# A two-model stack on one Trainium2 core: the RWKV inverses and their transposes part ways, and the mixers get new orders

## What is computed

```python
for l in range(DEPTH):                                   # DEPTH = 2
    h = rmsnorm(x, norm_g[l])
    proj = h @ w_in[l]                                   # all inputs of the three mixers
    y_a = hgrn2_mixer(a_q, a_ff, a_fb, a_i, ...) * silu(a_g)
    y_b = retention_mixer(b_q, b_k, b_v, ...) * silu(b_g)
    y_c = rwkv7_mixer(c_s, ...) * silu(c_g)
    mixed = gates_a * (y_a @ w_branch_a[l]) + gates_b * (y_b @ w_branch_b[l]) + gates_c * (y_c @ w_branch_c[l])
    x = x + mixed @ w_out[l]
```

```python
sa = einsum("bhvk,bhk->bhv", S, -kk_t)
S  = S * w_t + sa * (kk_t * a_t) + v_t * k_t
o  = einsum("bhvk,bhk->bhv", S, r_t)
```

## Time and profile before

| | |
|---|---|
| runs before | 3254.1, 3262.1, 3264.2 us, median 3262.1 |
| profiled execution, first to last instruction (span) | 3255.5 us |
| PE busy | 3046.9 us (94%) |
| DVE, ACT, POOL busy | 1688.1, 695.8, 260.2 us |
| chain that ended last, share on PE | 82% |

### The profile page before, as it was taken

How to read it: one execution, slowest core, us unless ns; L and a number is a source line. 1 busy time by engine, 2 the same in 40 slices (tenths; PEclk the granted TensorE clock), 3 DMA queues, 4 the chain that set the end, 5 groups by cost and what they waited for, 6 DMA issues and landing times.

```text
span 3255.5 us, 45292 instructions
## 1 busy us (share of the span) xinstructions
PE 3046.9 (94%) x18996; PEld 2523.1 (78%) x18996; DVE 1688.1 (52%) x3491; ACT 695.8 (21%) x1346; POOL 260.2 (8%) x326
## 2 busy tenths in 40 slices
PE   8989997989999989998899999999989979997999
PEld 7878886878886878887778887895759659764794
DVE  3556646355311564655555420773347557646575
ACT  3223423232111333323133110200110021013100
POOL 1201121020000121202012000000000000000000
PEclk9999998999999999999999999999989989996999
DMA  5323322324333423332233334444325425521343
GB/s 212 105 79 127 94 90 93 116 85 121 117 134 134 128 73 115 94 106 107 68 107 114 118 106 169 140 171 156 130 94 170 167 84 169 172 98 69 134 170 124
DMA packets 153754, 395.56 MB, mean 122 GB/s; under 512 B 90288, under 2 KB 106800, under 8 KB 109648
## 3 DMA queue, kind: packets, MB, share of 16 engines
q1 hardware_dynamic: 51376, 367.94, 32.6%
q10 hardware_dynamic: 100608, 19.93, 3.2%
q0 software_dynamic: 1568, 4.79, 0.4%
HBM read 380.04 MB, written 12.59 MB: 121 GB/s over the span
## 4 chain that ended last, share of the span: by engine, by line
PE 82%; DVE 10%; DMA 5%; ACT 2%; issue 1%; ACTq 1%; POOL 0%; DVEq 0%; SPq 0%
PE bank L418 25%; PE bank L1924 17%; PE bank L1942 7%; PE bank L1748 6%; PE bank L435 5%; PE bank L1811 4%; PE bank L1351 2%; DMA xT_scratch<-rw_bm 1%; PE bank L1953 1%; DMA rw_ex<-xT_scratch 1%; PE bank L731 1%; PE bank L750 1%; DVE rw_ex L662 1%; DVE rw_scored_a L1166 1%; DMA scores_scratch<-rw_scored_a 1%
## 5 line engine op out<-in xcount | busy, mean ns | idle before, releaser
L418 PE MATMUL bank<-h_features,weight_ring 128*128 128x256 f32 x4256 | 974.3, 385 | 10.8 <-DMA weight_ring<-in_w_in 4.8
L418 PEld LDWEIGHTS bank<-h_features,weight_ring 128*128 128x128 f32 x4256 | 805.0, 192 | 125.5 <-issue 6.1
L435 PE MATMUL bank<-weight_ring,h_features 128*128 128x256 f32 (+2 forms) x896 | 201.2, 375 | 3.1 <-DVE h_features L510 2.0
L435 PEld LDWEIGHTS bank<-weight_ring,h_features 128*128 128x128 f32 x896 | 161.9, 190 | 27.3 <-issue 2.3
L1924 PE MATMUL bank<-h_features,weight_ring 128*128 128x128 f32 x1408 | 171.9, 275 | 5.4 <-DVE h_features L510 5.4
L1924 PEld LDWEIGHTS bank<-h_features,weight_ring 128*128 128x128 f32 x1408 | 164.3, 192 | 6.1 <-DVE h_features L510 6.1
L1993 ACT COPY mem_normed<-bank 128x128 f32<-128x128 f32 x88 | 23.4, 265 | 482.7 <-PE bank L1924 482.7
L1748 PE MATMUL bank<-y_features,weight_ring 128*128 128x256 f32 x512 | 119.0, 382 | 0.0
L2076 DVE TENSOR_TENSOR mem_normed<-mem_normed,bank 128x256 f32<-128x256 f32 x88 | 37.0, 421 | 132.5 <-PE bank L1924 132.5
L1748 PEld LDWEIGHTS bank<-y_features,weight_ring 128*128 128x128 f32 x512 | 95.1, 190 | 13.0 <-issue 0.7
L1924 PE MATMUL bank<-y_rwkv_features,y_features 128*128 128x128 f32 x704 | 93.0, 275 | 0.0
(11 more groups left out here) (521 smaller groups left out, 4990.3 us busy)
## 6 DMA issues: line engine op xcount, KB each, us to landing
weight_ring<-in_w_in SPq DMA_DIRECT2D x146, 1024.0 KB, 4.9
weight_ring<-in_f00w SPq DMA_DIRECT2D x33, 1024.0 KB, 4.9
weight_ring<-in_f01w SPq DMA_DIRECT2D x33, 1024.0 KB, 4.8
weight_ring<-in_f10w SPq DMA_DIRECT2D x33, 1024.0 KB, 4.8
weight_ring<-in_f11w SPq DMA_DIRECT2D x33, 1024.0 KB, 4.9
weight_ring<-in_w_b SPq DMA_DIRECT2D x16, 1024.0 KB, 5.0
weight_ring<-in_w_out SPq DMA_DIRECT2D x16, 1024.0 KB, 4.9
weight_ring<-in_conv_in SPq DMA_DIRECT2D x10, 1024.0 KB, 4.9
```

Source lines behind the costliest of these rows:

```text
L418: m = e.matmul(bank[:, j, :], w[:, k, j * P:(j + 1) * P], x[:, k, :], start=k == 0, stop=k == kt - 1, skip_group_check=True)
L435: m = e.matmul(bank[:, t * n:(t + 1) * n], x[:, k, t * P:(t + 1) * P], w[:, k, :], start=k == 0, stop=k == kt - 1, skip_group_check=True)
```

## The change

Three things change.

1. The transposes get semaphores of their own (`rw_xT_stored_sem`, `rw_xT_sem`, and `rw_x_stored_sem`, `rw_x_sem` for the inverses), and `x` and `xT` swap their buffers: `x` is loaded into `rw_ex`, out of which it was stored, and `xT` into `rw_bm`. So neither exchange waits for the other.
2. Store and loads of the transposes leave ACT's queue for SP's, as a fourth stream X in SP's order. L741 (now L742) waits for them; L731 waits for `x` alone.
3. All orders of both mixers' stages are replaced, on five engines; both layers now have the same one. The second block's orders stay.

```diff
-    R.prod, R.x, R.xT = (flat(z).rearrange("p (n s) -> p n s", s=HALF_ROWS) for z in (R.sig, R.bm, R.ex))
+    R.prod, R.x, R.xT = (flat(z).rearrange("p (n s) -> p n s", s=HALF_ROWS) for z in (R.sig, R.ex, R.bm))
...
         if lv == BLOCK:
-            e.wait_ge(g.rw_inverse_sem, 64 * ((4 * l + q) * 2 + d + 1))
+            e.wait_ge(g.rw_x_sem, 32 * ((4 * l + q) * 2 + d + 1))
...
             e.wait_ge(*act.at("prod", *U, lv))
+            e.wait_ge(g.rw_xT_sem, 32 * ((4 * l + q) * 2 + d + 1))
             for i, rows in parts:
...
+def rwkv_inverse_sp(e, g, l):
+    S, R = g.rw, g.R
+    for q in range(4):
+        for d in range(2):
+            unit = (4 * l + q) * 2 + d
+            e.wait_ge(*S.dve.at("inverse", l, q, d))
+            e.wait_ge(g.rw_zeros_sem, 32)
+            if unit:
+                e.wait_ge(g.rw_xT_sem, 32 * unit)
+            e.dma_start(scratch_blocks(g.xT_scratch), block_rows(R.inv)).then_inc(g.rw_xT_stored_sem, 16)
+            yield
+            e.wait_ge(g.rw_xT_stored_sem, 16 * (unit + 1))
+            for half, rows in enumerate(ROW_HALVES):
+                e.dma_start(R.xT[rows], scratch_halves(g.xT_scratch, half)).then_inc(g.rw_xT_sem, 16)
             yield
...
-                e.wait_ge(g.rw_inverse_sem, 64 * unit)
-            e.dma_start(scratch_blocks(g.x_scratch), block_rows(R.inv_tmp)).then_inc(g.rw_stored_sem, 16)
-            e.dma_start(scratch_blocks(g.xT_scratch), block_rows(R.inv)).then_inc(g.rw_stored_sem, 16)
-            yield
-            e.wait_ge(g.rw_stored_sem, 32 * (unit + 1))
-            for z, scratch in ((R.x, g.x_scratch), (R.xT, g.xT_scratch)):
-                for half, rows in enumerate(ROW_HALVES):
-                    e.dma_start(z[rows], scratch_halves(scratch, half)).then_inc(g.rw_inverse_sem, 16)
+                e.wait_ge(g.rw_x_sem, 32 * unit)
+            e.dma_start(scratch_blocks(g.x_scratch), block_rows(R.inv_tmp)).then_inc(g.rw_x_stored_sem, 16)
+            yield
+            e.wait_ge(g.rw_x_stored_sem, 16 * (unit + 1))
+            for half, rows in enumerate(ROW_HALVES):
+                e.dma_start(R.x[rows], scratch_halves(g.x_scratch, half)).then_inc(g.rw_x_sem, 16)
...
         weave(g, f"mixers{l}", "sync", {
             "R": chain(rwkv_sp(e, g, l), branch_sp(e, g, l, 2, "w_c", 1)),
+            "X": rwkv_inverse_sp(e, g, l),
```

Of the order table one line, SyncE's of layer 0, as it now reads at its start:

```diff
-        "H R4 H4 B6 H5 R4 B6 H5 B5 R4 B H B H B H B H B H B3 R4 B4 H2 B H B2 H B H B H B H2 B R8 ",
+        "R4 H5 B5 X2 B H4 R X2 R3 B H B7 X2 B2 H2 X2 R4 H2 B H B4 X B2 X B H2 R X2 R3 H3 B7 X2 B6 H2 X H X2 R2 H "
```

More of the change, by code:

```diff
@@ L218 @@
     ("mixers0", "gpsimd"):
-        "H R3 H11 R H5 R2 H16 R H9 R2 H7 R H11 R2 H5 R ",
+        "H R3 H9 R H7 R2 H9 R H7 R2 H7 R H9 R2 H10 R H7 ",
     ("mixers1", "gpsimd"):
-        "R H R2 H11 R H5 R2 H16 R H10 R2 H6 R H11 R2 H5 R ",
+        "H R3 H9 R H7 R2 H9 R H7 R2 H7 R H9 R2 H10 R H7 ",
     ("mixers0", "sync"):
-        "H R4 H4 B6 H5 R4 B6 H5 B5 R4 B H B H B H B H B H B3 R4 B4 H2 B H B2 H B H B H B H2 B R8 ",
+        "R4 H5 B5 X2 B H4 R X2 R3 B H B7 X2 B2 H2 X2 R4 H2 B H B4 X B2 X B H2 R X2 R3 H3 B7 X2 B6 H2 X H X2 R2 H "
+        "R H R H R H R H2 R3 ",
     ("mixers1", "sync"):
-        "R4 H5 B6 H5 R4 B6 H5 B5 R4 B H B H B H B H B H B3 R4 B6 H4 B2 H B H2 B H B R8 ",
+        "R4 H5 B5 X2 B H4 R X2 R3 B H B7 X2 B2 H2 X2 R4 H2 B H B4 X B2 X B H2 R X2 R3 H3 B7 X2 B6 H2 X H X2 R2 H "
+        "R H R H R H R H2 R3 ",
     ("conv", "sync"):
@@ L3115, in __init__ @@
             nc.dram_tensor(n, (TT * 4 * HEAD_STRIDE,), F32).ap() for n in ("scores_scratch", "x_scratch", "xT_scratch"))
-        self.rw_scores_sem, self.rw_blocks_sem, self.rw_stored_sem, self.rw_inverse_sem, self.rw_zeros_sem = (
-            self.sem(n) for n in ("scores_stored", "blocks_loaded", "inverses_stored", "inverses_loaded",
-                                  "scratch_cleared"))
+        self.rw_scores_sem, self.rw_blocks_sem, self.rw_zeros_sem = (
+            self.sem(n) for n in ("scores_stored", "blocks_loaded", "scratch_cleared"))
+        self.rw_x_stored_sem, self.rw_x_sem, self.rw_xT_stored_sem, self.rw_xT_sem = (
+            self.sem(n) for n in ("inverses_stored", "inverses_loaded", "transposes_stored", "transposes_loaded"))
         self.vectors_sem, self.masks_sem = self.sem("vectors_loaded"), self.sem("masks_loaded")
```

## The result

The changed kernel takes 3293.95 us (median of 14 runs, 3280.94 to 3306.31), the kernel before 3266.73 us (14 runs, 3254.11 to 3286.69) on the same chips. The ratio is 1.008, with a 95% interval of 1.006 to 1.0099. The forecast was 3244 us. The time lies outside the forecast range too, 12 us above its upper end.

A forecast was written before the change was run, and what follows sets the result against it. PE was taken as the bound, busy 3046.9 of 3255.5 us. Stalls at L731 (-8), matmuls laid elsewhere (+2) and fewer changes of run (-3) gave -9 us a layer, -18 in all: 3244 us, range 3216 to 3282.

The forecast's parts named there:

- for those some 4 us it can't start a weight load: SP's queue: waiting for the inversion keeps weight loads off the inverse's store or load, taken as 2.0 us a unit.
- Term A: PE's stalls at L731: from 31.9 to 23.9 us a layer as the chain shortens, -8 us a layer.
- slower rival: Exchange: only issue time is saved, no collision spared; chain 25.1 us, kernel at 3272; chance 0.23.
- The clock ... 0, with 5 us either way.: PE's half clock: two stretches a layer before, three shorter ones after; effect 0, with 5 us either way.
- Term A's base: Modelled stalls at L731 before, with a chain of 27.5 us: 31.9 us a layer.
- term B: Matmuls laid elsewhere: other waits end, -13.4 us, against a new hole and thinner cover, +15; +2 us a layer.
- The new hole: Unit q = 1, d = 1, at L835: PE stalls 9.7 to 12.7 us for operands, taken as 11.
- ACT's 48 issues fewer: ACT's queue: 31 us of issue time less wins nothing, since ACT's waits hide it.
- three signs of being wrong: Loads of `x` landing after 5 us in half the units; L742 waiting; HGRN2 waiting on DVE over 10 us a layer.
- The planner's case: Exchange: transfers near their medians, chain 21.1 us, L731 stalls 13.5 us a layer, kernel at 3224; chance 0.17.

The follow-up runs named there:

- e1: Kernel before with the new orders alone, the exchange still joint and on ACT's queue: 3359.42 us, ratio 1.0285.
- e11: Changed kernel plus one wait on SP's queue, behind the transposes' loads, until the inverses' loads have landed: 3235.47 us, ratio 0.9905.
- e9: Changed kernel, transposes on ACT's queue, SP waiting until the inverses are loaded, one weight load ahead of the transposes' store's old place: 3210.61 us, ratio 0.9826.
- e4: Changed kernel with idle-filling matmuls, 49 a layer ahead of L731's waits and 30 ahead of two HGRN2 waits: 3280.75 us, ratio 1.0039.
- e7: Changed kernel with the loads of w_in after the tenth cut to a sixteenth, so its weights are wrong: 3218.16 us, ratio 0.9853.
- e10: Changed kernel with transposes on ACT's queue, before's orders, and SP waiting at the inversion's place until the inverses are loaded: 3240.54 us, ratio 0.9916.
- e8: Changed kernel with transposes on ACT's queue and SP waiting, where the transposes' store stood, until the inverses are loaded: 3213.84 us, ratio 0.9836.

## Why the prediction was wrong

The sum said -18 us; the span says +47.3 (by the medians, 3244 was forecast and 3293.95 measured, a miss of 50 us; the rest is the spread named above). Of the miss of 65 us, 42 are busy time (36.1 more in the two stages where -6 was forecast), 25 idle time (12.9 more where -12 was forecast), and -2 lie outside the stages.

**The step that failed: "for those some 4 us it can't start a weight load".** Term A rested on 2.0 us a unit of spared collisions. None was spared: 14 of 16 units are hit, for 7.0 us, where it was 12 and 5.4. The sum took the exchange from 9.1 to 4.7 us; measured, it went from 11.5 to 10.8. From the scores to L731 it is 25.6 us, 2.2 less than before, but only 0.7 of that is the exchange. Another 0.9 lies ahead of the inversion's end (15.6 us from the scores before, 14.7 after, 14.6 in e1 with the old exchange), and 0.6 is that PE now starts L731 as soon as `x` lands. So the slower rival's chain (25.1) is near by its number, and its argument from the Trainium skill (DMA: Bandwidth & Descriptors, Issuing engines are not separate DMA queues) held in that no collision was spared; but more and slower collisions ate most of the 2.4 us of issue time too. I looked at where SP waits, and not at when its wait ends against when `x` lands: 3 us after the inversion against 10.8. e11 and e9 show that keeping weight loads away does shorten the exchange: with the wait it takes 9.3 and 6.6 us, and the scores to L731 24.1 and 22.3.

**"The clock ... 0, with 5 us either way."** The largest error in size: 35 us. Up to some 20 of them are the spread of single executions. I priced the half clock by counting two stretches a layer before; the clock record of before has eight in layer 0 and seven in layer 1. The new orders put a wait at L731 into all 16 units and a hole of 11.9 us into both layers, and the time at the lower level nearly doubled (116 to 222 us). e4 (own matmuls 37.6 us shorter with the stalls filled), e7 (41.1), e11 (42.9) and e9 (45.0) all give this time back.

**Term A's base.** I set 31.9 us of stalls a layer at L731 for before, by a model, where the earlier trace rows has 6.5. In the units with thin cover PE was standing at HGRN2's waits inside the very stretch, and these hid the chain. PE in time before, ahead of the second unit's L731 (idle time in brackets):

```profile
186.62 0.80 PE L1365 MATMUL bank<-hg_vt,hg_at 128*128 128x128 f32 x2 [5.37 <-DVE hg_at L1513]
...
196.02 0.66 PE L1291 MATMUL bank<-float_constants,hg_bf 128*128 128x128 f32 x4 [3.65 <-DVE hg_bf L1531]
196.61 1.12 PE L731 MATMUL bank<-rw_bm,rw_scored_a 64*64 64x32 f32 x32
```

9.0 of the 13.4 us that I had put down to L731 in this unit are these two. For after the model gave 23.9 us a layer, and 24.3 was measured in layer 0, 54.7 in both. That 23.9 and 24.3 agree is luck: unit by unit the model has 2.2, 12.1, 0.1, 2.0, 5.4, 1.9, 0 and 0.2 us, and the trace 1.8, 1.0, 1.3, 3.2, 8.5, 3.8, 3.6 and 1.1. So term A was +18 us in layer 0, not -8. Against that, term B was better than +2: all other idle time of layer 0 fell by 12.8 us, from 49.3 to 36.5. The two errors are in part one: the same wait stood in both terms under different names.

**What held.** The new hole: forecast 11 us and at L835, measured 11.9 at the same place, though most of it under the name of L1367, which stands ahead. (11 lies nearer the undisturbed row, 9.7, than the disturbed, 12.7, other than the forecast says; measured from L820's end to L835 the operands took 15.9 us, the disturbed row's 15.6.) L742 never waited for the transposes. The weights are not late, and ACT's 48 issues fewer made no difference that can be seen. Two of the three signs of being wrong came true: the later load of `x` takes over 5 us in 12 of 16 units, and L1367 waits for DVE 15.0 us in layer 0. The planner's case was no fancy either: with a chain of 22.3 us e9 is 0.9% faster than e10, which has a hold and the orders of before (3210.61 against 3240.54 us); the changed kernel merely does not produce that chain.

## What to carry to other kernels

A transfer moved to another queue is not out of the way, and a wait on a queue protects only what ends before that wait does: ask what that queue issues next, and whether the transfer that an engine stands at has landed by then. Where a short transfer is on the critical path and long ones have tens of microseconds of slack, hold the long ones with one wait until the short one has landed; this was worth 1.7% here (e11 against the changed kernel), and nothing under orders that cover the transfer anyway (e10). Orders planned for the shortest chain lost much where the chain came out longer (e1: 2.9%), because on PE a stall was paid twice, once as a wait and once in matmuls at half clock. When comparing two orders by a model, put the old one's modelled stalls beside its measured waits first; here 31.9 against 6.5 would have told.

## What the runs showed of the hardware

- The half clock about doubled the price of idle time here, or more, with a wide spread. From the changed kernel to e9, PE's idle time falls by 49.0 us and the busy time of the same 18996 matmuls by 45.0; to e11, by 24.0 and 42.9; to e1, both rise, by 22.3 and 35.0. (The changed kernel's profiled execution is 10.6 us above its median, which swells the second figure of the first two.)
- A transfer of 64x8x64 elements lands in 2.7 to 4.0 us when no weight load is under way (e9, 32 transfers) and in up to 9.9 us beside them (e11); a small exchange on another queue at the same time costs 1.4 us of some 8.
- Putting the transposes on SP did not change what is moved, only which queue carries it. The page's queues, before and after (packets, MB, share of 16 engines' span):

```profile
q1 hardware_dynamic: 51376, 367.94, 32.6%
q10 hardware_dynamic: 100608, 19.93, 3.2%
```

```profile
q1 hardware_dynamic: 84912, 373.19, 33.2%
q10 hardware_dynamic: 67072, 14.69, 2.2%
```

The transposes' 33536 packets joined the queue that carries the weights. The best kernel of this study is e9, with e8 not told apart from it: 3210.61 us, 1.7% faster than before (0.9799 to 0.9852).
